# First LayerNorm's scale and shift rows of a decoder trunk, spread over the partitions by TensorE

## Chip, cores and metric

The kernel runs on one NeuronCore of a Trainium2 chip, out of eight. The metric is the device time of one launch in microseconds; lower is better. Weights and activations are fp32 in device memory.

## What is computed

A trunk of two layers over 256 tokens of width 1024. What matters here is its start: the first LayerNorm, with a scale row `ln_in_g` and a shift row `ln_in_b` of 1024 elements each, and what layer 0 takes from it.

```python
h = layer_norm(x, ln_in_g, ln_in_b)
for l in range(DEPTH):
    mix = hybrid_mixer(h, w_in[l], w_out[l], ...)
    h = layer_norm(DEEPNORM_ALPHA * h + mix, ln_mix_g[l], ln_mix_b[l])
    ffn = grouped_moe(h, w_router, router_bias, w_gate[l], w_up[l], w_down[l])
    h = layer_norm(DEEPNORM_ALPHA * h + ffn, ln_ffn_g[l], ln_ffn_b[l])
```

`hybrid_mixer` begins with `p = h @ w_in`; one part of `p` goes through a sigmoid gate into a causal depthwise convolution of 31 taps, others into attention and a gated unit. `grouped_moe` sends each token to two of 16 experts.

## The kernel before

Each engine has its own program, written out by hand, and they meet by semaphores. A partition holds a token (two blocks `b` of 128) or a channel.

**How weights come.** SyncE (SP) issues nearly all transfers, in one queue. A ring of nine units of 2 MB takes the weights in the order of use: per layer five column slabs of `w_in` and two of `w_out` (units 0 to 6, `load_slab`, L363 to L378), then six units for each of eight pairs of experts (`load_pairs`, L380 to L402). A transfer into a unit that was used before waits for the semaphore `used`, which TensorE raises. Unit 0 is special: it comes as two halves of 1 MB (L373 and L376), and between them stand the two rows of the first LayerNorm, each spread by the transfer itself to all 128 partitions (L374 and L375: 512 KB written for each 4 KB row, into `ln_par`). Ahead of unit 0 come the input `x` (L344), a table with the identity (`tab`, L345) and the per-channel columns `col_par` (L347 to L349); behind it small parameters (L353 to L361) and unit 1 (L378).

**The start of layer 0.** VectorE (DVE) takes the statistics of `x` (L1175 to L1184), GpSimd (POOL) the inverse deviation (L1085), and DVE writes the centred, scaled tokens into `normal` (L1198). TensorE (PE) keeps itself busy with 18 products that nobody reads (`keep_clock`, L465, `KEEP_START`), then turns `normal` to channels (`turn`, L473). ACT (L890) and DVE (L1218) evict the turned blocks from PSUM and apply scale and shift as columns from `col_par`, so this path does not need `ln_par`. PE multiplies by unit 0 (L707, 32 products in 64 passes: the gate and the value of the convolution, into banks 4 and 5). Meanwhile ACT makes a rounded copy of the turned tokens (`xi_hi`, L899), DVE the rest (`xi_lo`, L1228).

**The first split.** For unit 1 on, the projection runs as three products of a high and a low part. ACT makes the high part of seven chunks as soon as unit 1 has landed (`in_w_high`, L909), DVE the low part (`in_w_low`, L1236). In ACT's program the sigmoid of the gate (L997) stands behind these seven, with its function table's load. DVE's gate product (L1453) waits for the sigmoid and for `h_ready`; then DVE runs the 62 convolution steps (L1466, L1470), with the low parts of the other nine chunks between them, for which PE's products (L527) wait.

**The rows.** Only POOL reads `ln_par` here: `gain_and_shift` (L1100, L1103) makes `h` from `normal`, two passes for each block of tokens, for the residual sum. It waits for both rows (`par_in`) and for `norm_ready`, and raises `h_ready`.

**Around it.** Layer 1 begins in the same way (turn, L707, sigmoid, gate product), with the rows and its units loaded long before.

Of the kernel before, what the change touches and what calls it, by code (L numbers as in the profile page):

```python
# [9 lines left out]
ACT = mybir.ActivationFunctionType  # L10
# [7 lines left out]
P = 128  # L18
SEQ = 256
TB = SEQ // P  # L20
D = 1024
# [23 lines left out]
BANK = 512  # L45
# [15 lines left out]

KEEP_START, KEEP_MIX, KEEP_ROUTER, KEEP_SLOTS, KEEP_TURN = 18, 6, 18, 6, 18
COMB_BANKS, LAST_COMB_BANKS = (7, 4, 7, 4), (7, 4, 2, 3)


# [33 lines left out]
def trunk(nc, x, ln_in_g, ln_in_b, w_in, w_out, sg_ln_g, sg_ln_b, sg_w, sg_b, conv_w, conv_b,  # L101
          conv_ln_g, conv_ln_b, ln_mix_g, ln_mix_b, w_router, router_bias, w_gate, w_up, w_down,
          ln_ffn_g, ln_ffn_b, table, out):
    with ExitStack() as ctx:
        def sb(name, shape, dt=F32):
            return ctx.enter_context(nc.sbuf_tensor(name, [P] + shape, dt))

        def sem(name):
            return ctx.enter_context(nc.semaphore(name))

        bank = [ctx.enter_context(nc.psum_tensor(f"bank{i}", [P, BANK], F32)) for i in range(8)]
# [14 lines left out]
        area_b = sb("area_b", [3072])  # L126
# [7 lines left out]
        ln_par = sb("ln_par", [2, D])  # L134
# [50 lines left out]
        taps_rows = area_a[0:DEPTH * TAPS + DEPTH, 1024:1280]  # L185
        sgb_rows = area_a[0:DEPTH * GROUPS, 1280:1408]
        orders = area_b[:, 0:3 * P]
        cmp = area_b[:, 2048:2048 + 2 * TB * EXPERTS * PER_GROUP].rearrange("p (i n) -> p i n", i=2)
        rt_e, score, biased, rank, sel = (
            area_b[:, 2304 + 32 * i:2336 + 32 * i].rearrange("p (b e) -> p b e", b=TB) for i in range(5))  # L190
# [30 lines left out]
        table_in = sem("table_in")  # L221
        setup_in = sem("setup_in")
        small_in = sem("small_in")
        par_in = sem("par_in")
# [6 lines left out]
        pool_const = sem("pool_const")  # L231
# [4 lines left out]
        setup_pe = sem("setup_pe")  # L236
# [91 lines left out]
        def unit_at(n):  # L328
            return ring[:, n % RING, :]

        def wait_unit(pe, n):
            pe.wait_ge(landed[n % RING], 16 * (n // RING + 1))

        def bcast_row(ap1d, n):

            return ap1d.rearrange("(a n) -> a n", a=1).to_broadcast([P, n])
# [5 lines left out]
        def _(sp):  # L342
            for b in range(TB):
                sp.dma_start(h[:, b, :], x[0, b * P:(b + 1) * P, :]).then_inc(x_in[b], 16)  # L344
            sp.dma_start(tab[:, :], table[:, 0:T_BEFORE]).then_inc(table_in, 16)  # L345
            for i, (src_in, src_mix, src_ffn) in enumerate(((ln_in_g, ln_mix_g, ln_ffn_g), (ln_in_b, ln_mix_b, ln_ffn_b))):
                sp.dma_start(col_par[:, 0, i, :], src_in.rearrange("(p c) -> p c", c=KC)).then_inc(col_par_in, 16)  # L347
# [15 lines left out]
            def load_slab(l, i, n):  # L363
                if n >= RING:
                    sp.wait_ge(used, n - RING + 1)
                dst = unit_at(n).rearrange("p (c n) -> p c n", c=KC)
                if i < 5:
                    src = w_in[l].rearrange("(p c) n -> p c n", c=KC)[:, :, SLAB_COLS[i]:SLAB_COLS[i] + BANK]
                else:
                    src = w_out[l].rearrange("(c p) n -> p c n", p=P)[:, :, (i - 5) * BANK:(i - 4) * BANK]  # L370
                if n == 0:

                    sp.dma_start(dst[:, :, CV:], src[:, :, CV:]).then_inc(first_half_in, 16)  # L373
                    sp.dma_start(ln_par[:, 0, :], bcast_row(ln_in_g, D)).then_inc(par_in, 16)  # L374
                    sp.dma_start(ln_par[:, 1, :], bcast_row(ln_in_b, D)).then_inc(par_in, 16)  # L375
                    sp.dma_start(dst[:, :, 0:CV], src[:, :, 0:CV]).then_inc(landed[0], 16)  # L376
                else:
                    sp.dma_start(dst, src).then_inc(landed[n % RING], 16)  # L378
# [32 lines left out]
            for l in range(DEPTH):  # L411
# [13 lines left out]
                n = sp.value_load(fullest[0:1, l:l + 1], min_val=0, max_val=SEQ)  # L425
# [17 lines left out]
        def _(pe):  # L443
# [18 lines left out]
            def keep_clock(at, n):  # L462

                for _ in range(n):
                    pe.matmul(bank[at][:, :], ones_bf[:, :], ones_bf[:, :].unsqueeze(1).to_broadcast([P, 4, P]),  # L465
                              start=True, stop=True)

            def turn(src, b):

                for half in range(2):  # L470
                    dst = bank[2 * b + half]
                    for c in range(4):
                        mm = pe.transpose(dst[:, c * P:(c + 1) * P], src[:, b, 4 * half + c::KC], ident)  # L473
                    mm.then_inc(tr_pe, 1)
# [216 lines left out]
            def layer(l):  # L691

                u0 = l * LAYER_UNITS
                for b in range(TB):
                    pe.wait_ge(norm_ready, 2 * TB * l + b + 1)
                    turn(normal, b)
                w = unit_at(u0).rearrange("p (c n) -> p c n", c=KC)
                for k in (2, 3, 0, 1):
                    if l == 0 and k == 2:
                        pe.wait_ge(first_half_in, 16)  # L700
                    elif k == (2, 0)[l == 0]:
                        wait_unit(pe, u0)
                    for n in range(KC):
                        c = n // 2 + 4 * (n % 2)
                        if k == 2:
                            pe.wait_ge((tr_act, tr_dve)[n % 2], TR * l + 4 * (TB - 1) + n // 2 + 1)
                        mm = pe.matmul(bank[4 + k // 2][:, (k % 2) * SEQ:(k % 2 + 1) * SEQ],  # L707
                                       w[:, c, k * P:(k + 1) * P], xT[:, c, :], start=n == 0, stop=n == KC - 1)
# [34 lines left out]
                for hp in range(HEADS // 2):  # L743
                    for par in range(2):
                        q = slice(par * HD, (par + 1) * HD)
                        mm = pe.matmul(bank[6 + par][:, hp * P:(hp + 1) * P], qkT[q, 0, hp, 0:P], qkT[q, 1, hp, 0:P],
                                       start=False, stop=True, skip_group_check=True)
# [8 lines left out]
                for hp in range(HEADS // 2):  # L756
                    for par in range(2):
# [3 lines left out]
                                       start=False, stop=True, skip_group_check=True)  # L761
# [37 lines left out]
                for hp in range(HEADS // 2):  # L799
                    pe.wait_ge((probT_dve, probT_act)[hp % 2], 3 * l + 2 + hp // 2)  # L800
                    for kb in range(TB):
                        for e in range(2):
                            hd = 2 * hp + e
                            i = 2 * e + kb
                            mm = pe.matmul(bank[1][e * HD:(e + 1) * HD, hp * P:(hp + 1) * P],
                                           v_rows[:, kb, hd * HD:(hd + 1) * HD], probT[:, 2 + hp, i * P:(i + 1) * P],
                                           start=kb == 0, stop=kb == 1)
# [27 lines left out]
                for b in range(TB):  # L835
                    pe.wait_ge(strips_copied, TB * l + b + 1)
                    mm = pe.matmul(bank[5][:, 64 + b * EXPERTS:64 + (b + 1) * EXPERTS], part_logits[:, b, :], fold,
                                   start=True, stop=True)
# [28 lines left out]
                    more_rounds(l)  # L867
                    layers_from(l + 1)

            pe.wait_ge(pool_const, 3)  # L870
            keep_clock(5, KEEP_START)
            pe.wait_ge(table_in, 16)
            layers_from(0)


# [1 line left out]
        def _(act):  # L877
# [107 lines left out]
                                       scale=slot_gate[:, j % 2:j % 2 + 1]).then_inc(s["y_hi"], 1)  # L985

            act.preload_act_table(ACT.Identity)
            act.wait_ge(col_par_in, 16 * 6)
            for l in range(DEPTH):
                scaled_columns(3 * l, 2 * l, [(0, 0), (1, 0)])  # L990
# [7 lines left out]
                   .then_inc(sig_ready, 1)  # L998
                if l == 0:

                    act.wait_ge(setup_pe, 1)
                    nt = DEPTH * TAPS + DEPTH
                    act.activation(tapsT[:, :, :], bank[3][:, 0:CB * nt].rearrange("p (c k) -> p c k", c=CB), ACT.Copy)\
                       .then_inc(taps_copied, 1)
                    act.activation(sgbT[:, :], bank[3][:, 256:256 + DEPTH * GROUPS], ACT.Copy).then_inc(setup_copied, 1)
# [3 lines left out]
                for dst, g, s in ((cv_ln, conv_ln_g, conv_ln_b), (sg_ln, sg_ln_g, sg_ln_b)):  # L1009
                    act.dma_start(dst[:, 0, :], bcast_row(g[l], SG)).then_inc(rows_in, 16)  # L1010
                    act.dma_start(dst[:, 1, :], bcast_row(s[l], SG)).then_inc(rows_in, 16)
                act.wait_ge(setup_pe, l + 2)
                act.activation(sgwT, bank[5][:, :].rearrange("p (g t) -> p g t", g=GROUPS), ACT.Copy)\
                   .then_inc(setup_copied, 1)
                next_params(ln_mix_g[l], ln_mix_b[l], 2 * TB * l + TB)
# [53 lines left out]
                n = act.value_load(fullest[0:1, l:l + 1], min_val=0, max_val=SEQ)  # L1069
# [7 lines left out]
        def _(pool):  # L1077
# [10 lines left out]
            pool.memset(half_neg[:, :], -0.5).then_inc(pool_const, 1)  # L1088
            pool.memset(ones_bf[:, :], 1.0).then_inc(pool_const, 1)
            pool.memset(w_rt[:, :, EXPERTS:STRIP], 0.0).then_inc(pool_const, 1)  # L1090
            pool.wait_ge(pool_const, 3)
            inverse_deviations(TB)

            products = [0]
# [30 lines left out]
            for l in range(DEPTH):  # L1125
                if l:
                    pool.wait_ge(norm_ready, 2 * TB * l + TB)
                    for b in range(TB):
                        gain_and_shift(b, 2 * TB * l)
                pool.wait_ge(tr_pe, 4 * (3 * l) + 4)  # L1130
                pool.memset(glu[:, :, 0:PAD], 0.0).then_inc(pads_ready, 1)
                pool.wait_ge(sgw_in, 16 * (l + 1))
                pool.affine_select(out=sgw_rows, in_=sgw_rows, compare_op=ALU.is_ge, fill=0.0, base=0,
                                   pattern=[[0, GROUPS], [-1, P]], channel_multiplier=1).then_inc(sgw_masked, 1)
                if l == 0:
                    pool.wait_ge(small_in, 16 * 3)
                    pool.wait_ge(col_par_in, 16 * 6)
                    router_weights(0)
                pool.wait_ge(setup_pe, l + 2)
                rotate(l, 0)  # L1140
                rotate(l, 1)
                inverse_deviations(TB)
                inverse_deviations(TB)
                inverse_deviations(TB)
                pool.wait_ge(main_sems["pick"], TB * (ITERS * l + 1))
                for b in range(TB):
                    gain_and_shift(b, 2 * TB * l + TB)

                for b in range(TB):
                    pool.wait_ge(h_ready, 2 * TB * l + TB + b + 1)  # L1150
                    pool.tensor_scalar(acc[:, b, :], h[:, b, :], ALPHA, 1.0, ALU.mult, ALU.mult).then_inc(acc_init, 1)
                if l < DEPTH - 1:
                    pool.wait_ge(shift_pe, 1)
                    router_weights(l + 1)
                inverse_deviations(TB)
# [434 lines left out]
```

## Time and profile before

| | |
|---|---|
| median of 3 runs | 691.44 us (691.26 to 691.76) |
| profiled execution, its own time | 691.46 us |
| its span, first to last instruction | 689.6 us |
| busy, PE / DVE / ACT / POOL | 658.3 / 321.0 / 166.7 / 71.2 us |
| mean granted clock of PE | 0.994 |
| moved by transfers | 240.70 MB, mean 349 GB/s |

The span is the time from the first to the last instruction on the core; the execution's own time is 1.86 us longer. Busy times say little about the start of the program, where each engine waits for others; there the chain of waits, the timelines of the engines and the times of landing are read. In these, times count from the start of the span. A matmul of fp32 operands shows as two passes, each with its own load of stationary data (PEld).

### The profile page before, as it was taken

To read this page: it belongs to the slowest core of one execution; us is meant where nothing else is said; L and a number is where in the kernel's file an instruction comes from. 1 tells how busy PE (TensorE), PEld (TensorE's weight loads), DVE (VectorE), ACT (ScalarE), POOL (GpSimd) and SP (SyncE) were. 2 spreads that over 40 slices of the span, in tenths; PEclk is the share of its full clock that TensorE was granted. 3 is DMA by queue.
4 is the path that set the end of the run, shared out by engine and by line. 5 is a ranking of instruction groups with operands and counts; after the bars stand their busy time and mean duration, and the time that the engine had idled before them with its cause. 6 is when DMAs were issued, how large, how long until landed. Compare 5 with 4: busy or idle time off the path is not lost.

```text
span 689.6 us, 7631 instructions
## 1 busy us (share of the span) xinstructions
PE 658.3 (95%) x3105; PEld 339.1 (49%) x3105; DVE 321.0 (47%) x614; ACT 166.7 (24%) x324; POOL 71.2 (10%) x67
## 2 busy tenths in 40 slices
PE   8989999999999999998989999989999999999992
PEld 5854587543333553332478557855333436333331
DVE  6898877610321312320589978682220330320327
ACT  3511753231110221101153138424101114101100
POOL 3503100420000000000070040006000000000001
PEclk9999999999999999999999999999999999999997
DMA  8999936099999999999999973335999999999991
GB/s 286 366 390 414 387 124 244 1 360 397 428 431 428 426 429 427 429 423 419 401 382 395 419 314 123 122 123 208 363 420 428 431 426 429 426 428 429 416 407 66
DMA packets 39580, 240.70 MB, mean 349 GB/s; under 512 B 4524, under 2 KB 8948, under 8 KB 24180
## 3 DMA queue, kind: packets, MB, share of 16 engines
q1 hardware_dynamic: 36756, 236.49, 84.4%
q10 hardware_dynamic: 2784, 3.67, 1.5%
q8 instruction: 26, 0.43, 0.3%
q14 instruction: 14, 0.11, 0.0%
HBM read 239.10 MB, written 1.05 MB: 348 GB/s over the span
## 4 chain that ended last, share of the span: by engine, by line
PE 73%; DVE 11%; DMA 10%; ACT 2%; SPq 1%; issue 1%; POOL 0%; DVEq 0%; POOLq 0%; ACTq 0%
PE bank L591 22%; PE bank L624 10%; DMA ring<-in_w_up 8%; PE bank L495 8%; PE bank L509 6%; PE bank L569 5%; PE bank L606 5%; PE bank L660 4%; PE bank L639 4%; DVE mix L1470 4%; PE bank L707 2%; DMA ring<-in_w_in 2%; DVE in_lo L1236 2%; PE bank L614 1%; PE bank L779 1%
## 5 line engine op out<-in xcount | busy, mean ns | idle before, releaser
L591 PE MATMUL bank<-ring,xe 128*64 128x512 f32 x768 | 167.4, 593 | 0.0
L1397 DVE TENSOR_TENSOR area_b<-area_b,bank 128x512 f32<-128x512 f32 x16 | 11.0, 688 | 230.7 <-PE bank L591 166.6
L591 PEld LDWEIGHTS bank<-ring,xe 128*64 128x64 f32 x768 | 54.8, 137 | 108.3 <-issue 107.8
L624 PE MATMUL bank<-ring,area_b 128*64 128x512 f32 x384 | 85.0, 595 | 0.0
L1417 DVE SCALAR_TENSOR_TENSOR y_lo<-bank,slot_gate,y_hi 128x512 fp32r<-128x512 f32 x32 | 24.0, 750 | 87.7 <-ACT y_hi L984 87.7
L1085 POOL TENSOR_TENSOR rstd<-var_eps,half_neg 128x1 f32<-128x1 f32 x18 | 11.8, 661 | 510.1 <-DVE var_eps L1184 510.1
L606 PE MATMUL bank<-ring,xe 128*64 128x512 f32 x256 | 57.0, 595 | 3.4 <-DMA ring<-in_w_up 2.6
L495 PE MATMUL bank<-ring,xT_area 128*128 128x512 f32 x128 | 55.9, 592 | 0.0
L624 PEld LDWEIGHTS bank<-ring,area_b 128*64 128x64 f32 x384 | 26.5, 137 | 50.0 <-issue 50.0
L1470 DVE SCALAR_TENSOR_TENSOR mix<-mix,tapsT 128x256 f32<-128x256 f32 x120 | 49.8, 476 | 0.0
L984 ACT ACTIVATE y_hi<-bank,slot_gate 128x512 fp32r<-128x512 f32 x32 | 22.0, 687 | 98.4 <-PE bank L624 70.7
L1380 DVE TENSOR_TENSOR h<-h,bank 128x512 f32<-128x512 f32 x64 | 41.1, 678 | 1.7 <-PE bank L660 1.7
L509 PE MATMUL bank<-w_split,x_hi 128*128 128x512 f32 x128 | 39.7, 391 | 0.2
L974 ACT ACTIVATE area_b<-bank 128x256 f32<-128x256 f32 x16 | 6.2, 385 | 132.4 <-PE bank L577 132.4
L495 PEld LDWEIGHTS bank<-ring,xT_area 128*128 128x128 f32 x128 | 23.9, 190 | 27.7 <-issue 27.7
L606 PEld LDWEIGHTS bank<-ring,xe 128*64 128x64 f32 x256 | 17.7, 137 | 39.9 <-issue 33.0
L962 ACT ACTIVATE xe<-bank,col_par 128x512 f32<-128x512 f32 x32 | 24.9, 779 | 44.8 <-PE bank L569 44.8
L971 ACT ACTIVATE area_b<-bank 128x512 f32<-128x512 f32 x16 | 9.6, 597 | 90.9 <-PE bank L591 67.5
L660 PE MATMUL bank<-y_hi,back 128*128 128x512 f32 x64 | 29.1, 455 | 1.9 <-DVE y_lo L1417 1.9
L639 PE MATMUL bank<-ring,area_b 128*64 128x512 f32 x128 | 28.3, 595 | 1.6 <-DVE area_b L1403 1.6
L569 PE MATMUL bank<-pick,n_hi 128*128 128x512 f32 x64 | 29.8, 466 | 0.0
L707 PE MATMUL bank<-xT_area,ring 128*128 128x256 f32 x128 | 28.1, 380 | 1.2 <-ACT xT_area L890 1.2
(173 smaller groups left out, 857.7 us busy)
## 6 DMA issues: line engine op xcount, KB each, us to landing
ring<-in_w_gate SPq DMA_DIRECT2D x32, 2048.0 KB, 19.9
ring<-in_w_up SPq DMA_DIRECT2D x32, 2048.0 KB, 20.6
ring<-in_w_down SPq DMA_DIRECT2D x32, 2048.0 KB, 20.7
ring<-in_w_in SPq DMA_DIRECT2D x9, 2048.0 KB, 17.9
ring<-in_w_out SPq DMA_DIRECT2D x4, 2048.0 KB, 20.2
ring<-in_w_in SPq DMA_DIRECT2D x2, 1024.0 KB, 7.7
h<-in_x SPq DMA_DIRECT2D x2, 512.0 KB, 4.0
ln_par<-in_ln_mix_g ACTq DMA_DIRECT2D x2, 512.0 KB, 17.0
```

Source lines behind the costliest of these rows:

```text
L495: mm = pe.matmul(dst[:, :], xT[:, c, b * P:(b + 1) * P], w[:, c, :], start=c == 0, stop=c == KC - 1)
L509: mm = pe.matmul(bank[4 + 2 * b + n][:, :], x[:, k0, b * P:(b + 1) * P], w[:, part, :], start=k0 == 0 and k == 0, stop=k0 == KC - 1 and k ...
L569: mm = pe.matmul(bank[c % 2][:, :], part[:, b, c::KC], pick[:, b, :], start=b == 0 and part is n_hi, stop=b == TB - 1 and part is n_lo)
L591: mm = pe.matmul(bank[2 + m][e * SLOTS:(e + 1) * SLOTS, :], xe[:, k, at + e * SLOTS:at + (e + 1) * SLOTS], w[e][:, k * DE:(k + 1) * DE], s ...
L606: mm = pe.matmul(bank[2 + u % 2][e * SLOTS:(e + 1) * SLOTS, :], xe[:, k, at + e * SLOTS:at + (e + 1) * SLOTS], w[:, e, c, :], start=k == 0 ...
L624: mm = pe.matmul(bank[5 + n][e * SLOTS:(e + 1) * SLOTS, :], hidT[:, k, e * SLOTS:(e + 1) * SLOTS], w[e][:, k * D + n * BANK:k * D + (n + 1 ...
L639: mm = pe.matmul(bank[5 + n][e * SLOTS:(e + 1) * SLOTS, :], hidT[:, k, e * SLOTS:(e + 1) * SLOTS], w[:, e, c, n * BANK:(n + 1) * BANK], st ...
L660: mm = pe.matmul(bank[banks[k]][:, :], back[:, b, :], part[:, n * BANK:(n + 1) * BANK], start=part is y_hi, stop=part is y_lo)
L707: mm = pe.matmul(bank[4 + k // 2][:, (k % 2) * SEQ:(k % 2 + 1) * SEQ], w[:, c, k * P:(k + 1) * P], xT[:, c, :], start=n == 0, stop=n == KC ...
L962: act.activation(xe[:, c, :], bank[c % 2][:, :], ACT.Identity, scale=col_par[:, 2 * l + 1, 0, c:c + 1], bias=col_par[:, 2 * l + 1, 1, c:c ...
L1380: dve.tensor_tensor(a, a, bank[banks[k]][:, :], ALU.add).then_inc(s["added"], 1)
L1470: ins = dve.scalar_tensor_tensor(out=conv[:, cb, :], in0=src, scalar=tap, in1=conv[:, cb, :], op0=ALU.mult, op1=ALU.add)
```

## The change

The two rows come as 4 KB each into partition 0 of `ln_par`, right behind `x` in SP's queue and counted on `table_in`; the two spread transfers between the halves of unit 0 are gone. POOL writes a row of ones into partition 0 (`ones_row`, in a part of `area_b` that is free then). PE, after nine idle products in place of 18 and once the table and both rows are there, multiplies the row of ones with each half of each row (four products of one row, 128 columns out, 512 moving columns, fp32) into banks 6, 7, 4 and 5. ACT copies each bank into its half row of `ln_par`, ahead of everything else in its program but its table load, and the four copies raise `par_in` to the same 32 as the two transfers did. PE waits for that before the first product with unit 0, since that writes banks 4 and 5. The counts of `setup_pe` and `pool_const` follow.

```diff
-KEEP_START, KEEP_MIX, KEEP_ROUTER, KEEP_SLOTS, KEEP_TURN = 18, 6, 18, 6, 18
+ROW_HALVES = [(i, n) for i in range(2) for n in range(2)]
+ROW_BANKS = (6, 7, 4, 5)
+KEEP_START, KEEP_MIX, KEEP_ROUTER, KEEP_SLOTS, KEEP_TURN = 9, 6, 18, 6, 18
...
+        ones_row = area_b[0:1, 3 * P:4 * P]
...
             for b in range(TB):
                 sp.dma_start(h[:, b, :], x[0, b * P:(b + 1) * P, :]).then_inc(x_in[b], 16)
+            for i, row in enumerate((ln_in_g, ln_in_b)):
+                sp.dma_start(ln_par[0:1, i, :], row.rearrange("(a n) -> a n", a=1)).then_inc(table_in, 16)
             sp.dma_start(tab[:, :], table[:, 0:T_BEFORE]).then_inc(table_in, 16)
...
                     sp.dma_start(dst[:, :, CV:], src[:, :, CV:]).then_inc(first_half_in, 16)
-                    sp.dma_start(ln_par[:, 0, :], bcast_row(ln_in_g, D)).then_inc(par_in, 16)
-                    sp.dma_start(ln_par[:, 1, :], bcast_row(ln_in_b, D)).then_inc(par_in, 16)
                     sp.dma_start(dst[:, :, 0:CV], src[:, :, 0:CV]).then_inc(landed[0], 16)
...
                 w = unit_at(u0).rearrange("p (c n) -> p c n", c=KC)
+                if l == 0:
+                    pe.wait_ge(par_in, 32)
...
-            pe.wait_ge(pool_const, 3)
+            pe.wait_ge(pool_const, 4)
             keep_clock(5, KEEP_START)
-            pe.wait_ge(table_in, 16)
+            pe.wait_ge(table_in, 16 * 3)
+            for (i, n), at in zip(ROW_HALVES, ROW_BANKS):
+                pe.matmul(bank[at][:, :], ones_row, ln_par[0:1, i, n * BANK:(n + 1) * BANK],
+                          start=True, stop=True).then_inc(setup_pe, 1)
             layers_from(0)
...
             act.preload_act_table(ACT.Identity)
+            for k, ((i, n), at) in enumerate(zip(ROW_HALVES, ROW_BANKS)):
+                act.wait_ge(setup_pe, k + 1)
+                act.activation(ln_par[:, i, n * BANK:(n + 1) * BANK], bank[at][:, :], ACT.Copy).then_inc(par_in, 8)
...
+            pool.memset(ones_row, 1.0).then_inc(pool_const, 1)
```

How the programs stand at their starts, in SP's queue first, before (`h` is where `x` lands):

```order
L344 DMA h<-in_x 128x1024 x2
L345 DMA tab<-in_table 128x352
...
L373 DMA ring<-in_w_in 128x8x256
L374 DMA ln_par<-in_ln_in_g 128x1024
L375 DMA ln_par<-in_ln_in_b 128x1024
L376 DMA ring<-in_w_in 128x8x256
```

and in the changed kernel, whose own line numbers the rows have:

```order
L347 DMA h<-in_x 128x1024 x2
L349 DMA ln_par<-in_ln_in_g 1x1024
L349 DMA ln_par<-in_ln_in_b 1x1024
L350 DMA tab<-in_table 128x352
...
L378 DMA ring<-in_w_in 128x8x256
L379 DMA ring<-in_w_in 128x8x256
```

Two issues moved ahead of the table, the columns and the first half of unit 0, and two of 512 KB left the place ahead of its second half.

On PE, at the start of the program, before (`mix` is `normal`, `xT_area` the turned tokens):

```order
L465 MATMUL bank<-ones_bf 128x512 [waits pool_const]
L465 MATMUL bank<-ones_bf 128x512 x17
L473 MATMUL bank<-tab,mix 128x128 [waits norm_ready,table_in]
...
L707 MATMUL bank<-xT_area,ring 128x256 [waits tr_act,first_half_in]
```

and in the changed kernel (`area_b` holds the row of ones):

```order
L468 MATMUL bank<-ones_bf 128x512 [waits pool_const]
L468 MATMUL bank<-ones_bf 128x512 x8
L879 MATMUL bank<-ln_par,area_b 128x512 [waits table_in]
L879 MATMUL bank<-ln_par,area_b 128x512 x3
L476 MATMUL bank<-tab,mix 128x128 [waits norm_ready]
...
L712 MATMUL bank<-xT_area,ring 128x256 [waits tr_act,first_half_in,par_in]
```

The four products stand between the idle products and the turning of the tokens, and the first product with unit 0 has one more wait. On ACT, four copies (L998, `ln_par` from a bank) stand ahead of the eviction of the turned tokens.

## Rows read from the trace of the kernel before

**Rows 1.** The chain of waits: start us, us, what.
```profile
11.48 12.15 DMA ring<-in_w_in
23.65 0.45 ACT in_hi L909
...
28.72 0.61 ACT area_a L997
29.35 0.70 DVE mix L1453
...
52.59 13.73 PE bank L495 x32
```
**Rows 2.** Timeline of SP's issues: start us, us, line, what, count.
```profile
1.71 0.43 SPq L345 DMA_DIRECT2D tab<-in_table  x1
2.18 0.43 SPq L347 DMA_DIRECT2D col_par<-in_ln_in_g  x1
...
5.11 0.65 SPq L373 DMA_DIRECT2D ring<-in_w_in  x1
5.80 0.65 SPq L374 DMA_DIRECT2D ln_par<-in_ln_in_g  x1
6.49 0.43 SPq L375 DMA_DIRECT2D ln_par<-in_ln_in_b  x1
```
**Rows 3.** Issues of the first microseconds: count, KB each, median us to landing.
```profile
h<-in_x SPq DMA_DIRECT2D x2, 512.0 KB, 4.0
tab<-in_table SPq DMA_DIRECT2D x1, 176.0 KB, 4.4
...
ring<-in_w_in SPq DMA_DIRECT2D x1, 1024.0 KB, 5.8
...
ln_par<-in_ln_in_g SPq DMA_DIRECT2D x1, 512.0 KB, 6.5
ln_par<-in_ln_in_b SPq DMA_DIRECT2D x1, 512.0 KB, 7.1
```
**Rows 4.** Stretches: engines' busy us, granted clock, DMA share, GB/s.
```profile
6.00:7.00 1.00, 1.00 (x6) 0.48 (x5) 1.00 (x3) 0.00 (x0) 0.56 (x1) 1.00 0.32 41
...
7.00:24.00 17.00, 15.40 (x78) 13.08 (x77) 13.81 (x17) 5.14 (x11) 11.14 (x5) 1.00 1.06 351
...
121.00:130.00 9.00, 7.85 (x55) 4.12 (x54) 6.95 (x24) 1.70 (x4) 0.24 (x1) 1.00 0.01 2
```
**Rows 5.** Timeline of PE and PEld in the first 26 us.
```profile
1.23 6.28 PE L465 MATMUL bank<-ones_bf 128*128 128x512 bf16 x18 [1.23 <-POOL w_rt_gain L1090]
...
5.47 0.15 PEld L465 LDWEIGHTS bank<-ones_bf 128*128 128x128 bf16 x1 [0.28 <-issue]
...
5.83 1.18 PEld L465 LDWEIGHTS bank<-ones_bf 128*128 128x128 bf16 x6 [0.22 <-issue]
...
8.62 2.33 PE L473 MATMUL bank<-tab,mix 128*128 128x128 f32 x16 [1.11 <-DVE mix L1198]
...
11.40 14.05 PE L707 MATMUL bank<-xT_area,ring 128*128 128x256 f32 x64 [0.46 <-ACT xT_area L890]
```
**Rows 6.** The smallest PE product of the setup: ns min/median/max, start, form.
```profile
L451 PE MATMUL bank<-tab,area_a x1: 223/223/223, 25.7 to 25.7; 8*128 8x8 f32 x1
```
**Rows 7.** Timeline of ACT: the first eviction of turned tokens.
```profile
9.40 2.90 ACT L890 ACTIVATE xT_area<-bank,col_par 128x128 f32<-128x128 f32 x8 [7.32 <-PE bank L473]
```
**Rows 8.** Timelines at the start of layer 1: POOL, DVE, PE, ACT.
```profile
349.18 2.36 POOL L1100 TENSOR_TENSOR h<-mix,ln_par 128x1024 f32<-128x1024 f32 x1 [0.93 <-DVE mix L1198]
...
352.91 7.76 DVE L1228 TENSOR_TENSOR xi_lo<-xT_area,xi_hi 128x512 fp32r<-128x512 f32 x4 [0.80 <-ACT xi_hi L899]
...
351.02 14.05 PE L707 MATMUL bank<-xT_area,ring 128*128 128x256 f32 x64 [0.70 <-ACT xT_area L890]
...
365.11 0.60 ACT L997 ACTIVATE area_a<-bank 128x512 f32<-128x512 f32 x1 [6.37 <-PE bank L707]
```
**Rows 9.** Waits in the first 60 us: total us, times, longest.
```profile
PEld bank L527 <- DVE in_lo L1236: 5.1, 6, 1.0
```

More of the change, by code:

```diff
@@ L999, in _ @@
                 if l == 0:
-                    act.wait_ge(setup_pe, 1)
+                    act.wait_ge(setup_pe, len(ROW_HALVES) + 1)
                     nt = DEPTH * TAPS + DEPTH
@@ L1011, in _ @@
                     act.dma_start(dst[:, 1, :], bcast_row(s[l], SG)).then_inc(rows_in, 16)
-                act.wait_ge(setup_pe, l + 2)
+                act.wait_ge(setup_pe, len(ROW_HALVES) + l + 2)
                 act.activation(sgwT, bank[5][:, :].rearrange("p (g t) -> p g t", g=GROUPS), ACT.Copy)\
@@ L1090, in _ @@
             pool.memset(w_rt[:, :, EXPERTS:STRIP], 0.0).then_inc(pool_const, 1)
-            pool.wait_ge(pool_const, 3)
+            pool.memset(ones_row, 1.0).then_inc(pool_const, 1)
+            pool.wait_ge(pool_const, 4)
             inverse_deviations(TB)
@@ L1138, in _ @@
                     router_weights(0)
-                pool.wait_ge(setup_pe, l + 2)
+                pool.wait_ge(setup_pe, len(ROW_HALVES) + l + 2)
                 rotate(l, 0)
```

## Prediction

> **What bounds the start now.** I read the chain of waits first. Up to 11.48 us it is SP's issues; then 12.15 us of waiting for unit 1 of the weights; from 23.65 ACT splits seven chunks and loads the sigmoid's table; the sigmoid starts at 28.72 and the gate product at 29.35 [rows 1]. From there the convolution on DVE and PE's products hand the chain on without a wait for a transfer until the experts. So the place to look at is the start of the sigmoid, and two things meet in it: ACT must be through with the chunks of unit 1 (28.72 - 23.65 = 5.07 us after the landing), and PE must be through with L707. PE is through at 11.40 + 14.05 = 25.45 [rows 5], so 3.3 us of slack lie on PE's side, and the landing decides.
>
> Next I read what sets that landing. Between 7 and 24 us the DMA engines are busy without a gap (share 1.06, 351 GB/s), while from 6 to 7 us they moved 41 GB/s [rows 4]: the first half of unit 0, issued at 5.11 [rows 2], had not begun to flow. So the landing of unit 1 is the begin of that flow plus the bytes ahead of it. The first LayerNorm's rows are 1 MB of those bytes.
>
> Everything behind the sigmoid moves with it only if nothing else holds the rest of the program to the clock on the wall. Between 121 and 130 us the DMA engines do nothing (0.01) [rows 4]: the ring is full and waits for PE. The expert weights, which run at the limit later, therefore start when PE lets them, and a shift of PE goes through to the end. I count it in full, in both layers' experts.
>
> **The change, part by part, on the side of the transfers.** *Two issues more at the front.* Issues stand 2.18 - 1.71 = 0.47 us apart [rows 2]; the first half of unit 0 is issued two of them later, at 6.05, and since the engines idle ahead of it, the flow begins 0.94 us later. *Two spread transfers fewer.* The first half landed at 5.11 + 5.8 = 10.91, the first row at 5.80 + 6.5 = 12.30, the second at 6.49 + 7.1 = 13.59 [rows 2, 3]: together they held the engines 2.68 us. Net, unit 1 lands 1.74 us earlier, at 21.9, and ACT can start the sigmoid at 21.9 + 5.07 = 26.98. The bounds: if an issue's delay hides in the queue, 2.7 us earlier; if SP's queue is what holds unit 1 up, 0.94 us later.
>
> The 2.68 us come from this trace's landings. The Trainium skill ("DMA: Bandwidth & Descriptors", Specifications) gives a fabric ceiling of 435 GB/s, by which 1 MB would be worth an estimated 2.4 us, and the time below 690.0 instead of 689.7. The flow here ran at 351 GB/s, so I keep the landings.
>
> **On PE's side.** *When the products start.* They wait for the table. It landed at 1.71 + 4.4 = 6.11 [rows 2, 3]; now it is issued 0.94 us later, so 6.1 to 7.05. Ahead of it in the queue is x, two halves issued before 1.71, that land 4.0 us after issue in the middle [rows 3], so the second lands not long before the table: the table waited for x more than for its issue. I take 6.3, near the lower end. The two 4 KB rows are ahead of the table in the same queue and add little. The nine idle products end near 5.1: ten of them ran 0.43 us apart from 1.23 up to 5.47 [rows 5]. So PE stands still for about 1.2 us.
>
> *What they take.* No row has a product with one row of stationary data. From below there is the 8-row product of 8 columns, 0.22 us [rows 6]; from above a full product of 512 fp32 columns, two passes of 13.73 / 32 = 0.43 us (L495 [rows 1], 32 passes). The columns that stream through are the same 512, so I take the upper one: 8 passes, 3.43 us, and 0.2 for the first load. At PE's low rate it would be twice that (the rival below). The products end at 6.3 + 0.2 + 3.4 = 9.9; with both ends, 8.2 to 10.7.
>
> *What is queued behind.* The turning of the tokens started at 8.62 [rows 5] and now starts at 9.9, with both token blocks ready by then. From there to L707 it took 11.40 - 8.62 = 2.78 us, through ACT's eviction; L707 takes 14.05. So PE is through at 9.9 + 2.78 + 14.05 = 26.73, and the sigmoid follows at once, as in layer 1, where it starts at 365.11, 0.04 us after 351.02 + 14.05 [rows 8]. PE's side is thus 1.3 us later than before, at 26.8, and just about as late as the transfers' side, 26.98.
>
> *What costs nothing, and what covers it.* ACT's four copies: one from a bank of 512 columns takes 0.6 us (the sigmoid [rows 1]), shorter than the 0.86 of a product, so only the last stands behind the products, until 10.55. ACT's first eviction starts 9.40 - 8.62 = 0.78 us after the turning begins [rows 5, 7], at 10.68; without that margin it would cost up to 0.6. PE's new wait before L707 is over by then, 2.1 us early. POOL's memset of one row is short against its neighbours. POOL's passes over `h` start at 10.6 in place of 13.6, where the second row landed, and run beside DVE's eviction and split. Layer 1 has just that overlap: POOL starts at 349.18, and DVE's split ends at 360.67, 11.5 us later [rows 8]. Here that gives 22.1, about when unit 1 has landed and its first chunk is split; it does not hold up DVE. PE starts its split products (L527) 1.3 us later and should end them 1.74 earlier; the cover is the 5.1 us that their loads waited for DVE's low parts [rows 9], of which some 3 are used up.
>
> **The sum.** The sigmoid starts at the later of 26.98 and 26.8 in place of 28.72: 1.74 us earlier. The profiled execution's own time is 691.46, 0.02 above the median of 691.44, so I forecast **689.7 us**. With the products' start anywhere up to 7.05, and 0.4 us of doubt on the landing, 689.1 to 690.4.
>
> **The rivals.** *PE is still at its low rate when the products come (slower).* The granted clock reads 1.00 from 6 to 24 us [rows 4]; what came before it, the spacing tells: ten idle products 0.43 us apart (512 columns at 1.2 GHz), and from 5.83 six loads in 1.18 us (2.4 GHz) [rows 5]. PE had been busy for 4.4 us without a break when that came. Now it is busy for 3.9 and then stands still. If the rise does not come before the products, each microsecond of them at 1.2 GHz costs half a microsecond. It decides from the point where PE's side passes 28.72: the products end 11.85 or later, 1.95 us behind my figure, that is 3.9 us at the low rate. At the low rate throughout they take 6.9 us, end at 13.35, L707 at 30.2, and the kernel takes 691.46 + 1.5 = 693.0. If the rise comes while they run, 690 to 691.4. For it: half the idle products are gone and there is a gap. Against it: 3.9 us is nearly the 4.4 that sufficed. The Trainium skill ("TensorE: Matmul & The Clock Gate", Part 1) calls the low rate the default, that activity releases, and says that the point of release varies by run. By that rule the rival, in whole or part, would show in some runs; no row here shows a second start.
>
> *Unit 1 lands no earlier.* Small parameters on few engines stand ahead of it, and SP's issue of unit 1 at 11.48 [rows 1] might be what counts. Then the sigmoid stays or moves by the 0.94: 691.5 to 692.4. Against it: engines busy throughout, and 12.15 us between issue and landing for 2 MB.
>
> *The gain is given back.* The experts' weights run at the DMA limit; if that stream were held from its start by the queue and not by PE, nothing would move: 691.4. Against it the idle engines at 121 us.
>
> **Chances.** The forecast 0.62; PE partly at the low rate 0.18 and throughout 0.08; unit 1 not earlier 0.06; given back 0.06. A measurement of this kernel tells about 0.2%, 1.4 us, from no change; faster by more than that is under 690.06. Of the forecast's case most lies there, and a little of the partly slow one: 0.54. Slower by 0.2% is over 692.8, the low rate throughout and little else: 0.07. Within: 0.39. The range 689.1 to 691.4 holds the forecast and the partly slow case, some 0.8.
>
> **What would show it.** Right: unit 1's first split on ACT near 21.9; four products with 0.43 us for each pass, from about 6.3 to 9.9; L707 from about 12.7 to 26.7; the sigmoid near 27.0, and the rest of the chain with the same lengths as before. Wrong: passes 0.86 us apart; L707's end past 28.7; unit 1 landing at 23 or later; or an early sigmoid with the L707 of layer 1 still at 351.0 [rows 8], where 349.3 is expected.

## The result, and the profile after

The change made the kernel slower: 693.66 us median of 7 runs (692.83 to 694.67) against 691.82 of 7 runs of before (691.26 to 692.89), a ratio of 1.0024 with a 95% interval of 1.0013 to 1.0035. The forecast was 689.7, in a range up to 691.4. The profiled execution took 693.66, against 691.46.

The chain of waits of the changed kernel (start us, us, what) begins at another place than before [rows 1]: up to 60 us no transfer of weights is in it, and PE holds it from 6.4 us on.

```profile
2.36 3.99 DMA tab<-in_table
6.35 0.04 issue
6.39 7.19 PE bank L879 x8
13.58 3.36 PE bank L476 x16
16.94 0.03 issue
16.97 14.12 PE bank L712 x64
...
31.52 20.64 PE bank L530 x90
...
52.16 1.66 PE bank L530 x6
...
54.25 6.01 PE bank L498 x14
```

L879 is the four products in eight passes, L476 the turning of the tokens (L473 before), L712 the products with unit 0 (L707), L530 the split products (L527), L498 stands for L495. The products began as forecast (6.39 for 6.3) and took 7.19 us for 3.6. The turning took 3.36 us, L712 began at 16.97, 3.39 after the turning for 2.78, and ended at 31.09 for 26.73.

ACT's timeline of the changed kernel shows that the transfers' side did what was forecast: unit 1 was there at 21.45 (21.9 forecast, 23.65 before [rows 1]), the sigmoid's table was loaded at 26.5, and then ACT waited 4.63 us for PE.

```profile
21.45 0.63 ACT L917 ACTIVATE in_hi<-ring 128x512 fp32r<-128x512 f32 x1 [1.68 <-DMA ring<-in_w_in]
...
25.22 1.28 ACT L1008 ACT_TABLE_LOAD   x1
...
31.13 0.60 ACT L1008 ACTIVATE area_a<-bank 128x512 f32<-128x512 f32 x1 [4.63 <-PE bank L712]
```

The sigmoid at 31.13 is 2.41 us later than at 28.72, and the first L498, at 54.25 for 52.59 [rows 1], 1.66 later: 0.75 is given back between them. DVE's timelines, before and in the changed kernel, show where. Before, the first four convolution steps of this stretch took 0.75 us more than the four behind them; in the changed kernel every four take the same.

```profile
32.12 2.41 DVE L1470 SCALAR_TENSOR_TENSOR mix<-mix,tapsT 128x256 f32<-128x256 f32 x4
...
35.06 1.66 DVE L1470 SCALAR_TENSOR_TENSOR mix<-mix,tapsT 128x256 f32<-128x256 f32 x4
```

```profile
34.54 1.67 DVE L1482 SCALAR_TENSOR_TENSOR mix<-mix,tapsT 128x256 f32<-128x256 f32 x4
```

The longest of the slow steps took 0.86 us for 0.48, while POOL ran a mask, and a product for the router, from 32.59 to 34.25. In the changed kernel POOL ran these two from 31.26 to 32.48, beside DVE's wait for the sigmoid and its gate product. So this gain hangs on where the two engines happened to meet, and no run tests it alone. PE's split products, whose loads had waited 5.1 us for DVE's low parts [rows 9], now waited 0.4. PE and DVE end nearly level: DVE's last low part was done at 52.10, PE's last six products began at 52.16.

The 1.6 us then stay: L712 of layer 1 starts at 352.64 for 351.02 [rows 8]. The execution's own time is 2.20 longer; the last 0.6 appear where layer 1's experts wait for weights, 29.45 us in the chain of waits in place of 28.88. Why that wait is longer is not shown.

What the passes looked like, from the timeline of PE's weight loads in the changed kernel: 0.85 us apart. That is twice the 0.43 us that a pass of 512 fp32 columns takes at 2.4 GHz (L495 [rows 1]), so PE ran at 1.2 GHz.

```profile
7.41 0.33 PEld L879 LDWEIGHTS bank<-ln_par,area_b 1*128 1x128 f32 x1 [0.52 <-issue]
...
8.26 0.33 PEld L879 LDWEIGHTS bank<-ln_par,area_b 1*128 1x128 f32 x1 [0.52 <-issue]
...
11.67 0.33 PEld L879 LDWEIGHTS bank<-ln_par,area_b 1*128 1x128 f32 x1 [0.52 <-issue]
```

PE was busy with them for 7.2 us without a break, and its clock did not rise. It rose only about the end of the turning of the tokens, 3.4 us of products with 128 rows: L712 took 14.12 us, near the 14.05 of before [rows 5]. Before, 4.4 us of idle products were enough [rows 5]. That is what the experiments had to explain. The granted clock, the column behind the engines' busy times, is no help for the stretch ahead of its first change: it reads 1.00 there, in both kernels, as in this stretch of the changed one, in the middle of the slow passes.

```profile
12.00:13.00 1.00, 1.00 (x2) 0.01 (x1) 0.00 (x0) 0.57 (x1) 0.00 (x0) 1.00 1.10 352
```

### The profile page after: what moved, and what is told of

It reads as the page before. It is cut to its first block, busy times and chain, and to the rows that moved or that the text cites. A ratio compares the mean times of both kernels' runs of the same rounds, so it can differ in the third digit from the quotient of the medians.

```text
span 691.9 us, 7637 instructions
## 1 busy us (share of the span) xinstructions
PE 663.2 (96%) x3104; PEld 342.4 (49%) x3104; DVE 318.4 (46%) x614; ACT 169.4 (24%) x328; POOL 70.6 (10%) x68
## 4 chain that ended last, share of the span: by engine, by line
PE 79%; DMA 9%; DVE 8%; issue 1%; ACT 1%; POOL 0%; SPq 0%; DVEq 0%; POOLq 0%; ACTq 0%
PE bank L594 22%; PE bank L627 10%; DMA ring<-in_w_up 8%; PE bank L498 8%; PE bank L512 6%; PE bank L572 5%; PE bank L609 5%; PE bank L663 4%; PE bank L642 4%; PE bank L712 4%; PE bank L530 3%; DVE mix L1482 2%; PE bank L617 1%; PE bank L879 1%; PE bank L476 1%
## 5 line engine op out<-in xcount | busy, mean ns | idle before, releaser
L498 PE MATMUL bank<-ring,xT_area 128*128 128x512 f32 x128 | 55.9, 592 | 0.0
L627 PEld LDWEIGHTS bank<-ring,area_b 128*64 128x64 f32 x384 | 26.5, 137 | 50.0 <-issue 50.0
L498 PEld LDWEIGHTS bank<-ring,xT_area 128*128 128x128 f32 x128 | 23.9, 190 | 27.7 <-issue 27.7
L712 PE MATMUL bank<-xT_area,ring 128*128 128x256 f32 x128 | 28.2, 381 | 0.7 <-ACT xT_area L898 0.7
```

The lines of the kernel that those rows point to most:

```text
L498: mm = pe.matmul(dst[:, :], xT[:, c, b * P:(b + 1) * P], w[:, c, :], start=c == 0, stop=c == KC - 1)
L627: mm = pe.matmul(bank[5 + n][e * SLOTS:(e + 1) * SLOTS, :], hidT[:, k, e * SLOTS:(e + 1) * SLOTS], w[e][:, k * D + n * BANK:k * D + (n + 1 ...
```

## The experiments

Theory A: nine idle products are too few, and the pause behind them (5.4 to 6.4 us) breaks them off; the four products are products like others. Theory B: products with one row of stationary and moving data neither raise the clock nor hold it.

**e1_keep18**: 18 idle products again.

```diff
-KEEP_START, KEEP_MIX, KEEP_ROUTER, KEEP_SLOTS, KEEP_TURN = 9, 6, 18, 6, 18
+KEEP_START, KEEP_MIX, KEEP_ROUTER, KEEP_SLOTS, KEEP_TURN = 18, 6, 18, 6, 18
```

> The change with 18 idle products again in place of nine. Theory A (too few idle products and the pause of 1 us behind them left TensorE at its low rate; one-row products are like any others): the clock rises near 5.7 us inside the idle products, which end near 7.6; the eight passes stand 0.43 us apart and end near 11.2; L707 ends near 28.1, the sigmoid starts at 28.1 against 28.7 before; 0.6 us faster than before. Theory B (products with one row of stationary data do not count as work for the clock): the passes begin 0.43 us apart, but the clock falls during them or behind them, so that the turning of the tokens or the first passes of L707 run at the low rate; L707 ends later than 28.1, and the kernel is no faster than before.

**e2_keep13**: the same line with 13, meant to leave no pause and lose no time (in the profiled run the one-row products began at 7.01, without a pause).

> The change with 13 idle products, so that they end near 6.2 us, where the table lands, with no pause. Theory A: the clock rises near 5.7 us, the passes stand 0.43 us apart from 6.4 to 9.9, L707 ends near 26.8, the sigmoid starts near 27; 1.7 us faster than before. Theory B: the clock may rise by the idle products, but falls during or behind the one-row products, or does not rise at all before the turning of the tokens; sigmoid between 27.5 and 31.

Measured: e1 692.42 (691.34 to 694.08, 10 runs), ratio 1.0002 (0.9992 to 1.0011); e2 692.98 (691.07 to 693.96), ratio 1.0002 (0.9993 to 1.0012), both against 692.52. The profiled run of e1 went as A had it, in the timelines of PE and ACT: passes at the high rate, the turning in 2.05 us, the sigmoid at 28.10, and 691.34 us.

```profile
7.58 3.69 PE L879 MATMUL bank<-ln_par,area_b 1*128 1x512 f32 x8
11.20 2.05 PE L476 MATMUL bank<-tab,mix 128*128 128x128 f32 x16
14.01 14.05 PE L712 MATMUL bank<-xT_area,ring 128*128 128x256 f32 x64 [0.76 <-ACT xT_area L898]
...
28.10 0.60 ACT L1008 ACTIVATE area_a<-bank 128x512 f32<-128x512 f32 x1 [1.85 <-PE bank L712]
```

But A also forecast 0.6 us less than before, and the median is that of before. Five of the ten runs lie at 691.34 to 692.04, with a mean granted clock of 0.990 to 0.994, five at 692.79 to 694.08, with 0.988 to 0.990; of the second five there is no trace. The profiled run of e2 caught a fall of the clock. Its stretches (engines' busy us, then the granted clock, DMA share, GB/s) show PE busy throughout and the clock going to half at 10.5, behind 3.5 us of one-row products:

```profile
7.00:8.00 1.00, 1.00 (x4) 0.50 (x4) 0.93 (x4) 0.00 (x0) 0.02 (x1) 1.00 0.63 141
...
10.00:10.50 0.50, 0.50 (x2) 0.00 (x0) 0.00 (x0) 0.50 (x1) 0.00 (x0) 0.94 1.11 371
10.50:11.00 0.50, 0.50 (x2) 0.22 (x2) 0.00 (x0) 0.10 (x2) 0.00 (x0) 0.50 1.08 346
...
12.00:13.00 1.00, 1.00 (x7) 1.00 (x6) 0.13 (x1) 1.00 (x3) 1.00 (x1) 0.50 1.10 348
13.00:14.00 1.00, 1.00 (x7) 1.00 (x5) 1.00 (x4) 0.86 (x4) 1.00 (x1) 0.57 1.09 331
14.00:15.00 1.00, 0.98 (x6) 0.59 (x5) 0.97 (x4) 1.00 (x4) 0.92 (x2) 1.00 1.04 308
```

So the turning of the tokens fell into the low rate (3.45 us), and the sigmoid came at 28.42 for the 27 that A expected; even so this run, at 691.97, is one of the faster of e2. The clock was back before 14 us, and since the one-row products PE had run nothing but this turning, with 128 rows. A has no place for this; B has.

**e3_onerow_idle**: the kernel before, its idle products with one row.

```diff
-            keep_clock(5, KEEP_START)
+            for _ in range(KEEP_START):
+                pe.matmul(bank[5][:, :], ones_bf[0:1, :], ones_bf[0:1, :].unsqueeze(1).to_broadcast([1, 4, P]),
+                          start=True, stop=True)
```

> The kernel before, with its 18 idle products made of one row of stationary data and one moving row (same 128 columns out, same 512 columns through, same type). Theory A: spacing as before, 0.43 us up to about 5.5 us and 0.2 behind it; the time of before. Theory B: all 18 stand 0.43 us apart and end near 8.9, and the turning of the tokens runs at the low rate (3.4 us in place of 2.1 to 2.3); since the landing of unit 1 sets the sigmoid, the time hardly changes: 0 to 0.5 us.

Measured: 692.55 (692.36 to 692.73, 10 runs) against 692.52, ratio 0.9998 (0.9988 to 1.0008). The time tells nothing, as expected, since unit 1's landing covers it; the timelines of PE and its loads, in the one profiled run, do.

```profile
1.22 7.85 PE L872 MATMUL bank<-ones_bf 1*128 1x512 bf16 x18 [1.22 <-POOL w_rt_gain L1092]
9.01 3.68 PE L473 MATMUL bank<-tab,mix 128*128 128x128 f32 x16
12.48 14.49 PE L707 MATMUL bank<-xT_area,ring 128*128 128x256 f32 x64
...
7.60 0.14 PEld L872 LDWEIGHTS bank<-ones_bf 1*128 1x128 bf16 x1 [0.28 <-issue]
8.03 0.14 PEld L872 LDWEIGHTS bank<-ones_bf 1*128 1x128 bf16 x1 [0.28 <-issue]
```

All 18 stand 0.43 us apart up to the end, where full ones had gone to 0.2 from 5.83 [rows 5]. This is what B expects: same columns, same type, same count, one row in place of 128, and no rise in 7.85 us. How many rows would be enough was not tried.

**e7_keep9_only**: the kernel before with nine full idle products and nothing else (the line of e1, 18 to 9).

> The kernel before with nine idle products in place of 18 and nothing else. Theory A: nine full products and then a pause leave the clock low, the turning of the tokens at 8.6 takes 3.4 us instead of 2.3, L707 starts about 1.1 us later and its first passes may be slow; unit 1's landing still sets the sigmoid, so the time stays within 0.5 us. Theory B alone says nothing on it: if the turning runs at full rate here, nine idle products were enough and only the one-row products are to blame.

Measured: 692.75 (691.79 to 692.95, 10 runs) against 692.56, ratio 1.0004 (0.9995 to 1.0013). In the profiled run the turning took 3.65 us behind a pause of 3.49:

```profile
8.73 3.65 PE L473 MATMUL bank<-tab,mix 128*128 128x128 f32 x16 [3.49 <-DVE mix L1198]
```

So A holds in part: nine idle products and a pause can leave PE low as well. The pause is longer than the 1.0 us of the change, and the trace does not tell whether the clock never rose or rose and fell again; e5 and e10 below found it up behind the same nine products and pauses of 1.9 and 1.2 us. Alone, nine idle products cost no time that shows here.

**e5_full9, e6_full12, e9_full18**: the four products made full, with nine, 12 and 18 idle products. VectorE writes the zeros first, at the start, where it is idle; the rows come behind them, through ACT's queue and no longer through SP's.

```diff
-        ones_row = area_b[0:1, 3 * P:4 * P]
+        ones_row = area_b[:, 3 * P:4 * P]
...
-                pe.matmul(bank[at][:, :], ones_row, ln_par[0:1, i, n * BANK:(n + 1) * BANK],
+                pe.matmul(bank[at][:, :], ones_row, ln_par[:, i, n * BANK:(n + 1) * BANK],
...
+            pool.memset(ones_row, 0.0).then_inc(pool_const, 1)
+            pool.wait_ge(pool_const, 4)
+            pool.memset(ones_row[0:1, :], 1.0).then_inc(pool_const, 1)
...
+            dve.memset(ln_par[:, :, :], 0.0).then_inc(out_done, 1)
...
+            act.wait_ge(out_done, 1)
+            for i, row in enumerate((ln_in_g, ln_in_b)):
+                act.dma_start(ln_par[0:1, i, :], row.rearrange("(a n) -> a n", a=1)).then_inc(table_in, 16)
```

> The change with its four products made full: 128 rows of stationary data (a row of ones over 127 rows of zeros) against 128 moving rows (the scale or shift row over zeros, which VectorE writes first); nine idle products as in the change. The two rows come through ACT's queue, so SP's queue has no issue more than before the change. Theory B (one-row products do not count for the clock): the products now count; the clock rises while they run or before, the passes go from 0.86 to 0.43 us apart within them, the turning of the tokens takes 2.1 to 2.3 us; L707 ends between 26.5 and 28.3, the sigmoid at 26.6 to 28.4, 0.4 to 2 us faster than before. Theory A (nine idle products and the pause behind them are the cause): the passes stay 0.86 us apart as in the change, the products end near 13, and the sigmoid comes at 30 or later.

> The same with 12 idle products, which end near 6.2 us, where the table lands: no pause. Theory B: the clock rises at 5.5 to 6 us and stays in every run, as all products are full; passes 0.43 us apart from 6.3 to 9.8, L707 ends near 26.6, unit 1 lands near 20.9 and ACT is ready at 26.0, so the sigmoid starts near 26.7: 2.0 us faster than before, ratio 0.997, with runs that scatter no more than those of before. Theory A expects the same time; the scatter tells nothing on it. If zeros in the rows do not count either, as e2_keep13: scatter of 3 us, no gain.

> The pair to e1_keep18: 18 idle products, then the four products, but full (128 rows of stationary data and of moving data, zeros in all but one) in place of one-row. In the profile both look alike: passes 0.43 us apart from 7.6 to 11.1, sigmoid near 28.1, about 0.6 us faster than before. What differs is the scatter. If one-row products let the clock fall (theory B), the runs here lie close together, within 1.5 us, near 692.0 where before is at 692.5, and none reaches 693.5, as four of the ten of e1_keep18 did or nearly did. If the scatter of e1_keep18 had another cause (the later turning of the tokens, the idle time of PE behind it), it is here as well.

Measured: e5 692.71 (690.92 to 693.19, 11 runs), ratio 1.0002 (0.9993 to 1.0011); e6 691.32 (690.22 to 691.52, 11 runs), ratio 0.998 (0.9971 to 0.9989), both against 692.56; e9 691.26 (691.07 to 692.24, 11 runs) against 692.19, ratio 0.9986 (0.9977 to 0.9995). In e6 the rows landed later than I had counted (the memset comes first), at 6.9; from there it went as forecast for the change, in the timelines of PE and ACT:

```profile
6.90 3.67 PE L878 MATMUL bank<-ln_par,area_b 128*128 128x512 f32 x8 [1.24 <-DMA ln_par<-in_ln_in_b]
10.41 1.95 PE L474 MATMUL bank<-tab,mix 128*128 128x128 f32 x16
13.15 14.05 PE L710 MATMUL bank<-xT_area,ring 128*128 128x256 f32 x64 [0.80 <-ACT xT_area L897]
...
27.24 0.60 ACT L1010 ACTIVATE area_a<-bank 128x512 f32<-128x512 f32 x1 [1.36 <-PE bank L710]
```

The pair of e1 and e9 is the cleanest: in both profiles the passes stand 0.43 us apart, but e1's runs spread over 2.7 us and e9's over 1.2, all of e9's with a mean granted clock of 0.993 or more. In e9's timeline of PE:

```profile
7.13 3.67 PE L878 MATMUL bank<-ln_par,area_b 128*128 128x512 f32 x8
```

They differ also in the queue that brings the rows. That e1's slow runs come from a fall of the clock, as the one in e2's trace, is argued from their lower granted clock and not seen. Two numbers missed their forecast: e9's sigmoid came at 27.47 for 28.1, since its idle products reached the high rate at 4.9 us for 6.0 in e1, and e6's at 27.24 for 26.7, with the later rows. B had forecast 0.4 to 2 us less for e5, and its median shows none. It lies in two groups (four runs up to 691.73, seven from 692.5): full products do not always make up for nine idle ones and a pause of 1.9 us. Its profile shows only a run of the first group, with the passes 0.43 us apart from the first on and the sigmoid at 27.50; what the second group does is not shown.

**e10_after_again**: the change once more, beside e9.

> The change itself once more, on the same chip and against the same runs of before as e9_full18. Theory B: as measured first, 0.15 to 0.35% slower than before, and in the profile either the passes of the four products 0.86 us apart, or the clock high for them and fallen for the turning of the tokens; the sigmoid between 28.7 and 31.2.

Measured: 692.82 (692.7 to 694.48, 11 runs) against 692.19, ratio 1.0016 (1.0007 to 1.0025). Seven runs lie at 692.70 to 692.87, all with a mean granted clock of 0.988, four at 694.1 to 694.5. The profile is of the first kind: the clock had risen in the pause behind the idle products, and fell under the one-row products at 8.8. The stretches:

```profile
7.00:8.00 1.00, 1.00 (x4) 0.41 (x3) 0.93 (x4) 0.21 (x1) 0.05 (x1) 1.00 0.51 132
8.00:9.00 1.00, 1.00 (x4) 0.43 (x3) 0.59 (x1) 0.74 (x2) 1.00 (x1) 0.86 1.06 369
9.00:10.00 1.00, 1.00 (x3) 0.47 (x2) 0.81 (x1) 0.24 (x1) 0.01 (x1) 0.50 1.09 387
...
14.00:15.00 1.00, 1.00 (x6) 0.87 (x5) 1.00 (x4) 0.86 (x3) 0.92 (x2) 0.50 1.03 310
15.00:16.00 1.00, 1.00 (x5) 0.73 (x4) 0.74 (x4) 1.00 (x4) 1.00 (x1) 0.72 1.06 306
```

From 9 to 15 us it is 0.50; the sigmoid starts at 29.46. The first profile, with all passes at the low rate from the start and the sigmoid at 31.13, and its 693.66, look like the second kind, of which e10 has no trace.

Side by side, the ratios, each with an interval of some 0.001 to either side, show that the change has two faults of about the same size, its one-row products and its nine idle products. With one-row products: 1.0024 and 1.0016 with nine idle products, 1.0002 with 13 and with 18. With full ones: 1.0002 with nine, 0.998 with 12 and 0.9986 with 18. Among these six, mending either one brings the kernel back to the time of before; only mending both makes it faster.

**e4_no_rows**: what the transfers' side alone is worth. No row transfers and no products; the residual sum leaves out the first LayerNorm's scale and shift.

```diff
-                    sp.dma_start(ln_par[:, 0, :], bcast_row(ln_in_g, D)).then_inc(par_in, 16)
-                    sp.dma_start(ln_par[:, 1, :], bcast_row(ln_in_b, D)).then_inc(par_in, 16)
...
+            dve.memset(ln_par[:, 0, :], 1.0).then_inc(par_in, 16)
+            dve.memset(ln_par[:, 1, :], 0.0).then_inc(par_in, 16)
```

> The kernel before without its two row transfers and without any products for them: VectorE fills ln_par with ones and zeros while it is idle, so the residual sum leaves out the scale and shift of the first LayerNorm. It shows what the transfer side alone is worth: unit 1 lands near 20.9 us, ACT is ready for the sigmoid at 26.0, L707 ends at 25.5 as before; the sigmoid starts near 26.0, and the kernel is 2.7 us faster than before. If the gain were given back in the experts (rival), less than 1 us.

Measured: 689.72 (689.07 to 690.02, 4 runs) against 692.52, ratio 0.9955 (0.9939 to 0.9972), 2.8 us. ACT's timeline:

```profile
20.91 0.63 ACT L907 ACTIVATE in_hi<-ring 128x512 fp32r<-128x512 f32 x1 [6.65 <-DMA ring<-in_w_in]
...
25.97 0.60 ACT L995 ACTIVATE area_a<-bank 128x512 f32<-128x512 f32 x1
```

The sigmoid is 2.75 us earlier than before, and the time follows: no gain is lost in the experts.

**e8_fp32r**: one-row products in one pass each. ACT rounds the rows and the row of ones to fp32r, so the scale and shift of the first LayerNorm are rounded; 18 idle products; the rows leave SP's queue.

```diff
+            for i, row in enumerate((ln_in_g, ln_in_b)):
+                act.dma_start(ln_par[0:1, i, :], row.rearrange("(a n) -> a n", a=1)).then_inc(out_done, 16)
...
+            act.activation(ones_r[0:1, :], ones_row, ACT.Copy).then_inc(table_in, 16)
+            act.wait_ge(out_done, 32)
+            for i in range(2):
+                act.activation(rows_r[0:1, i, :], ln_par[0:1, i, :], ACT.Copy).then_inc(table_in, 16)
...
-                pe.matmul(bank[at][:, :], ones_row, ln_par[0:1, i, n * BANK:(n + 1) * BANK],
+                pe.matmul(bank[at][:, :], ones_r[0:1, :], rows_r[0:1, i, n * BANK:(n + 1) * BANK],
```

> One-row products, but in single passes: ACT copies the row of ones and the two rows (which come through ACT's queue) to the rounded fp32r type, so the first LayerNorm's scale and shift are rounded; 18 idle products as before. Four passes of 0.23 us from 7.6 to 8.6, in the gap that PE had before the turning of the tokens. Both theories: too short for the clock to fall in most runs; the turning starts near 8.7, L707 ends at 25.5, unit 1 lands near 20.9, the sigmoid starts at 26.0: 2.7 us faster than before, as e4_no_rows. If the clock falls behind even so short a stretch of one-row products, runs that scatter up to 1.5 us above that.

Measured: 689.45 (689.0 to 690.31, 5 runs) against 692.56, ratio 0.9963 (0.995 to 0.9977). The four products fit into the time in which PE waited before (in the profiled run they began at 6.83 for 7.6, since the idle products reached the high rate at 3.9 us), the turning starts at 8.64 as before [rows 5], and the sigmoid at 26.00:

```profile
6.83 1.19 PE L879 MATMUL bank<-rows_r,ones_r 1*128 1x512 f32 x4
8.64 2.42 PE L476 MATMUL bank<-tab,mix 128*128 128x128 f32 x16 [0.63 <-DVE mix L1217]
11.45 14.05 PE L712 MATMUL bank<-xT_area,ring 128*128 128x256 f32 x64 [0.39 <-ACT xT_area L898]
...
26.00 0.60 ACT L1015 ACTIVATE area_a<-bank 128x512 f32<-128x512 f32 x1
```

This is the best version that was run, at the price of the rounding; e6 and e9 keep fp32 and are also faster than before.

## Why the prediction was wrong

- **What bounds the start, and that a shift there goes through:** right in the main. The sigmoid is where the two sides meet; in e4 and e8 it starts 2.75 and 2.72 us earlier, and the kernel is 2.80 and 3.11 us faster. In the first profile of the change 2.41 us of delay became 2.20, by the 0.75 that DVE gave back and the 0.6 that the experts added, neither of which was in the forecast.
- **The transfers' side:** right. Unit 1 landed 2.2 us earlier for 1.74. SP's two issues cost less than counted: the first half of unit 0 was issued at 5.67 for 6.05.
- **When the products start:** right, 6.39 for 6.3.
- **What they take:** this step failed. "8 passes, 3.43 us" took the pitch of L495, a row from a stretch at 2.4 GHz, for a stretch whose clock was still to be earned. In the first profile the passes ran at 1.2 GHz throughout, 7.19 us, in e10 from 8.8 us on. The 2.78 us for the turning stood on the same rate, and it took 3.39. The products' price at a given clock was right: at the high rate four took 3.62 us in e1 with one row and 3.51 in e9 with 128.
- **The slower rival:** this is the case that came in the first profile, with 693.0 for 693.66. That the price is so near is partly luck: products and turning at the low rate took 0.9 us more than it had (it left the turning at 2.78), and the 0.75 of DVE and the 0.6 of the experts nearly cancel. I gave it 0.08 and put the upper end of the range below it. What misled me was the argument against it, "3.9 us is nearly the 4.4 that sufficed", and the belief that the rise could come while the products run; in e3 18 such products brought none. The case of e10, a clock that is up and falls under the products, stood in no rival. The Trainium skill ("TensorE: Matmul & The Clock Gate", Part 1) has the low rate as the default that activity releases; the traces agree: the full idle products begin 0.43 us apart in every one and go to 0.2 later, as at 5.83 before [rows 5], or not at all. That a PE busy throughout may fall to it, e2 and e10 show with a granted clock of 0.50.
- **POOL's overlap, ACT's four copies, PE's new wait:** ACT's copies waited for the products, as counted. POOL began at 14.44 in place of 10.6 for the same reason and held up nothing on the chain. The cover of the split products, 5.1 us of waits, was used up once PE's side was 5.6 us late; PE's products then became the chain, just ahead of DVE.

## What to carry to other kernels

An engine that is busy isn't by that kept at its clock: in these runs products with one row left PE at 1.2 GHz (e3, the change) or let it fall there (e2, e10), so they did not take the place of idle products, and what stands behind them must be priced at the low rate. Price moved work at the clock of the place it moves to, and where the clock changes nearby, make the low rate a case with a real chance. A broadcast by products can still pay when it is short: in e8 one pass in place of two fitted into a gap that PE had, and the 1 MB of transfers was then worth its full 2.7 us at the sigmoid.

## What the runs showed that was not expected

- One-row products neither brought PE's clock up nor kept it there: 18 of them over 7.85 us brought no rise (e3), and under four of them the granted clock fell to 0.50 with PE busy on them without a break (e2 at 10.5 us, e10 at 8.8).
- The rise comes at different times behind the same start: the weight loads of the idle products go to the short pitch at 3.9 us in e8, 4.6 in e6, 5.8 in before, and in e10 the rise came in the pause. A kernel whose start depends on it scatters: 692.7 to 694.7 for the change, in e10 in two groups 1.4 us apart. In the loads' timelines of e8 and e6:

```profile
3.90 2.34 PEld L468 LDWEIGHTS bank<-ones_bf 128*128 128x128 bf16 x11 [0.28 <-issue]
```

```profile
4.62 0.55 PEld L466 LDWEIGHTS bank<-ones_bf 128*128 128x128 bf16 x3 [0.28 <-issue]
```

- The granted clock reads 1.00 up to its first recorded change, also where the passes are at half rate; only their pitch tells.
